# Normed tile and arena moved against the weights' address modulo 512

## The reference

```
h = rmsnorm(x) * (1 + scale) + shift        # scale, shift, gate = silu(c) @ w_ada + b_ada
proj = h @ w_in                             # retention, state-space and forgetting-attention inputs, gates
mixed = concat(retention * silu(rg), rmsnorm(ssd * silu(z)), fox * silu(fg))
x = x + gate * (mixed @ w_out)
```

```
h = rmsnorm(x) * (1 + sc1) + sh1            # both streams
conv, mlstm, attention  from  h @ w_in      # N_IN = 8976 columns
x = x + g1 * ((g_conv*conv + g_mlstm*mlstm + g_attn*attn) @ w_out)
h = rmsnorm(x) * (1 + sc2) + sh2
x = x + g2 * ((a * silu(g)) @ w_down)       # a, g = dwconv(h @ w_up), D_FF = 2816
```

## Time and profile before

| | |
|---|---|
| median of three runs | 2268.26 us |
| the profiled execution | 2270.83 us |
| its span, first to last instruction | 2269.0 us |
| mean granted TensorE clock over the span | 0.983 of full speed |
| TensorE, VectorE, ScalarE, GpSimd busy | 97%, 74%, 43%, 5% |
| DMA, GB/s over the span | 143 |

### The profile page before, as it was taken

The page is one execution under the profiler, slowest core; times in us unless marked ns, Lnnn a source line. Parts: engine busy times, 40 slices in busy tenths (PEclk is TensorE's granted clock), DMA queues, the critical chain, the costliest instruction groups (busy, mean ns, idle before and its releaser), DMA issues.

```text
span 2269.0 us, 33300 instructions
## 1 busy us (share of the span) xinstructions
PE 2195.2 (97%) x13838; PEld 1879.1 (83%) x13838; DVE 1676.1 (74%) x3037; ACT 980.0 (43%) x1568; POOL 107.8 (5%) x86
## 2 busy tenths in 40 slices
PE   5999999999999999999999999999999999999999
PEld 4898888888878887778887688867789888999999
DVE  5887879777659686647874799966459766766984
ACT  3458533485533354453222333311344546544542
POOL 0000000000000121210000000000000313000000
PEclk9999999999999999999999999999999999999999
DMA  8954378443332111116562355635442212664553
GB/s 303 330 187 130 111 254 288 130 141 106 109 93 75 56 57 38 38 43 198 172 200 93 112 191 201 201 122 180 144 113 83 85 57 66 196 204 142 180 172 121
DMA packets 280807, 324.49 MB, mean 143 GB/s; under 512 B 28496, under 2 KB 261456, under 8 KB 280528
## 3 DMA queue, kind: packets, MB, share of 16 engines
q1 hardware_dynamic: 280656, 322.36, 44.1%
HBM read 321.29 MB, written 1.05 MB: 142 GB/s over the span
## 4 chain that ended last, share of the span: by engine, by line
PE 84%; DVE 11%; ACT 2%; DMA 2%; issue 1%; POOL 0%; SPq 0%; DVEq 0%; ACTq 0%
PE ps L754 83%; DVE parts L1951 2%; DVE ring L1908 2%; DMA ring<-w_ada_t 1%; ACT w_high L1412 1%; PE ps L1203 1%; DVE arena L2506 1%; DVE arena L2052 1%; DMA ring<-w_in 1%; DVE ada_dot L1908 0%; DVE arena L2097 0%; DVE parts L2320 0%; DVE arena L2103 0%; POOL parts L1854 0%; ACT arena L1524 0%
## 5 line engine op out<-in xcount | busy, mean ns | idle before, releaser
L754 PE MATMUL ps<-parts,w_high 128*128 128x256 f32 (+1 forms) x6512 | 1142.7, 325 | 8.4 <-ACT w_high L1412 6.2
L754 PEld LDWEIGHTS ps<-parts,w_high 128*128 128x128 f32 x6512 | 970.0, 190 | 123.1 <-issue 18.6
L754 PE MATMUL ps<-parts,parts 128*128 128x256 f32 (+1 forms) x3384 | 605.1, 320 | 9.2 <-DVE parts L1951 4.3
L1412 ACT ACTIVATE w_high<-ring 128x1024 fp32r<-128x1024 f32 (+2 forms) x442 | 439.5, 1012 | 298.3 <-PE ps L754 153.0
L754 PEld LDWEIGHTS ps<-parts,parts 128*128 128x128 f32 x3384 | 503.9, 191 | 61.8 <-DVE parts L1951 7.3
L2320 DVE TENSOR_TENSOR parts<-ring,w_high 128x1024 fp32r<-128x1024 f32 (+2 forms) x282 | 320.2, 1142 | 129.9 <-ACT w_high L1412 129.6
L1908 DVE CUSTOM_DVE_ANT_0 ring<-ring,c_rows,cols 128x1024 f32<-128x1024 f32 x144 | 183.1, 1278 | 20.7 <-DMA ring<-ada_w_t 8.8
L754 PE MATMUL ps<-arena 128*64 128x256 f32 (+7 forms) x928 | 184.8, 397 | 10.8 <-ACT arena L1494 7.8
L1854 POOL TENSOR_TENSOR parts<-ring,w_high 128x512 fp32r<-128x512 f32 x80 | 107.4, 1368 | 1821.9 <-ACT w_high L1412 1821.8
L754 PEld LDWEIGHTS ps<-arena 128*128 128x128 f32 (+2 forms) x928 | 122.9, 171 | 59.2 <-issue 19.0
L2349 DVE SCALAR_TENSOR_TENSOR arena<-arena,cols 128x512 f32<-128x512 f32 (+1 forms) x240 | 159.5, 664 | 6.2
(11 more groups left out here) (266 smaller groups left out, 1856.4 us busy)
## 6 DMA issues: line engine op xcount, KB each, us to landing
ring<-w_in SPq DMA_DIRECT2D x118, 1024.0 KB, 5.3
ring<-ada_w_t SPq DMA_DIRECT2D x48, 1024.0 KB, 5.0
ring<-ffn_w_up SPq DMA_DIRECT2D x44, 1024.0 KB, 5.1
ring<-w_ada_t SPq DMA_DIRECT2D x24, 1024.0 KB, 7.0
ring<-w_out SPq DMA_DIRECT2D x16, 1024.0 KB, 5.2
ring<-ffn_w_down SPq DMA_DIRECT2D x16, 1024.0 KB, 5.2
ring<-w_out SPq DMA_DIRECT2D x16, 512.0 KB, 4.7
ring<-w_mlstm_out SPq DMA_DIRECT2D x8, 1024.0 KB, 5.2
```

The lines of the kernel that those rows point to most:

```text
L754: return tensor.matmul(o, a, b, start=first, stop=last)
L1412: scalar.activation(half_high(m), half_raw(m), ACT.Copy).then_inc(*a.step(("w_high", m)))
```

## The change

Four allocations change their size; no instruction is added, removed or reordered.

```diff
-        LINE, ASIDE = 128, 48
+        LINE, ASIDE = 128, 64
+        sb("before_normed", [P, LINE - 16])
         laid = [0]
         one_high, one_low = under([P, KT, SEQ], KT * SEQ + ASIDE), under([P, KT, SEQ], ASIDE)
         laid.append(1)
         h_low = under([P, KT, TT])
         hT = sb("hT", [P, KT, TT])
-        sb("beside", [P, LINE])
+        sb("beside", [P, LINE + 16])
         laid.append(1)
         ring_low, h_keep = under([P, RING, KT * 256]), under([P, KT, TT], RING_OPEN * KT * 256)
         ring = sb("ring", [P, RING, KT * 256])
...
-        sb("before_arena", [P, -sum(n + -n % 8 for n in widths) % LINE])
+        sb("before_arena", [P, -sum(n + -n % 8 for n in widths) % LINE + 16])
```

## The result

Over 20 runs of each, the changed kernel takes 2273.43 us (2269.5 to 2275.94) and the kernel before 2268.46 us (2263.56 to 2272.47): a ratio of 1.0017, interval 1.0011 to 1.0024. The forecast was 2241, a ratio of 0.988.

What follows compares the result with a forecast made beforehand. TensorE, busy 97%, was taken to bound the kernel by its matmul pace. Savings of 30.6 us less 1.1 ("wo1"), 1.3 (VectorE) and 1.1 (waits) gave 27.1, so 2268.3 became 2241 us; range 2206 to 2274, the forecast's own 2228 to 2255.

Steps and rivals of the forecast that it cites:

- The failed step: Moved 512-column matmuls: the same 4.4 ns saved each as at 256 columns, within 6952 x 4.4 ns = 30.6 us.
- The mis-sized term: Moved 256-column matmuls at 64 or 448: 115.6 ns, the middle of 113.3 and 117.9, 4.4 ns saved each.
- rival A: All moved matmuls: 64 and 448 lock into 113.3 ns, 39.8 us saved, 2228 us; inside the forecast's 0.53.
- 117.9 everywhere: Rival A's opposite, all moved matmuls: 6952 x 2.1 = 14.6 us less 1.1, 2255 us; inside the forecast's 0.53.
- `mixed_low` at 256: Low pass of "wo1", 256 matmuls from 192 to 256: paced as at 0, 4.4 ns lost each, +1.1 us.
- the rule of odd and even 64-byte steps: Odd 64-byte steps from the weights (64, 448) taken like 192, even ones (256) like 0.
- Phase "one": First-block phase kept at distance 192: no change, 113 to 118 ns.
- VectorE's limit: Up stage of layer 0: VectorE nearly full, so 2.7 of 4.0 us saved counts and 1.3 us is lost.
- C: Rival for the whole kernel: no effect, 0 + 1.1 us, 2269 us; chance 0.17.
- D: Rival, all second-block strips slower: 6.7 ns a matmul, up to 47.7 us, 2316, most between 2275 and 2316; chance 0.17.
- B: Rival, all moved matmuls: free of collisions at 109.3 ns, 62 us saved, 2206 us; chance 0.13.
- The rule: Skill's two independent SBUF read ports: no address matters, sum 0; the trace disagreed by 6.7 ns.

Runs made afterwards that it cites:

- e1: A program of its own, only streams of 64 split matmuls, one distance and width each, some with lead-in matmuls or VectorE work; 1110.87 us.
- e7: A program of its own, streams of 72 split matmuls behind eight lead-ins, or with passes of 8 at different distances in turn; 829.9 us.
- e9: e4's kernel plus 16 matmuls at distance 0, eight ahead of the last layer's up stage and eight ahead of its down stage; 2257.39 us, ratio 0.9944.
- e8: The kernel of e4 run again unchanged, as the neighbour of e9 and e10; 2257.67 us, ratio 0.9953.
- e4: Kernel before, with the last layer's moving tiles for 2268 matmuls of 256 columns laid 64 bytes lower, distance 448; 2258.95 us beside 2267.53, ratio 0.996.
- e10: e4's kernel with the low parts of up and down in the last layer left at distance 0, turn (192, 192, 0); 2257.57 us, ratio 0.9946.
- e2: Kernel before, with the arena's tiles alone moved by 64 bytes and hT left in place; 2272.58 us, ratio 1.0007.
- e3: Kernel before, with the normed tile hT alone moved to distance 448 and the arena left at 0; 2271.49 us, ratio 1.0002.

## Why the prediction was wrong

The measured 2273.4 us lies within the stated range, 2206 to 2274, but at the end that was there for no effect. That it lies within is luck: no part of the forecast has losses that cancel gains.

**The failed step** is "with 512 columns the same, as the excess is the same". Two widths with 13.3 ns over their streaming time at distance 0 were taken as one cost with one remedy, and the 4.4 ns won at 256 columns were booked for 3436 matmuls of 512, 15 of its 31 us before deductions. At 512 columns the rows of before held distance 0 alone, so nothing there spoke on how it moves. Measured: +2.2 ns at 64 and +6.7 at 448 (e1), and in the kernel's up stage 3.9 more on the mean of both. That is 2540 x 2.2 + 896 x 6.7 = 11.6 us lost for 15.1 won, the whole sign of the result.

**The mis-sized term** is 256 columns: 115.6 ns taken, the middle of two paces; 117.9 measured. 64 and 448 both have two paces, 113.3 and 117.8, but in the turns of 64 and 448 the slower one stood, in the last layer's up stage and in e7's (64, 64, 448) after all four lead-ins. 3516 x 2.1 = 7.4 us won instead of 15.5. The opposite of rival A, "117.9 everywhere", was right here, but for `project_values`, whose pass on `h_low` between passes at 0 ran at 113.4.

**What was right.** `mixed_low` at 256 is as at 0: 120.0 ns after 116.3, 256 x 3.7 = +0.9 us. The reason given was not: the rule of odd and even 64-byte steps fails at 128, an even number, where e1 has 118.6 and 232.1, and 64 and 192 differ with 512 columns, 228.9 and 233.3. It is the period of 256 bytes that makes 256 as 0. Phase "one" stood. VectorE's subtractions, of the changed kernel (ns min, median, max):

```profile
L1998 DVE TENSOR_TENSOR parts<-hT,parts x16: 404/406/407, 65.9 to 347.3; 128x256 fp32r<-128x256 f32 x16
L2313 DVE TENSOR_TENSOR parts<-hT,parts x32: 419/686/694, 602.2 to 2086.0; 128x512 fp32r<-128x512 f32 x24, 128x256 fp32r<-128x256 f32 x8
```

These are the values of the earlier trace rows to within 3 ns. The sum by what was measured: 11.6 - 7.4 + 0.9 = +5.1 us, and the medians differ by 5.0; the good fit is partly luck, as `h_keep`'s neighbours, pauses and the granted clock are not in it and the first block's +1.1 us is only explained in part.

**A sum that was off.** The idle time before the five forms of the earlier trace rows adds to 18.7 us, not 16, and their busy time to 1806 us, not 1600. Nothing else hangs on it.

**VectorE's limit** in the up stage of layer 0 never came into play: there was nothing to give back, as the stage grew by 3.9 us.

**The rivals.** The time lies between C's 2269 and the 2275 from which most of D runs. C was wrong in the mechanism: addresses do matter, and gains and losses nearly cancel. D's price of 6.7 ns for a low pass 64 bytes off on the other side is the value measured, but for 512 columns alone, and not by its argument, since 64 itself costs 2.2. B's floor of 109.3 is reached at no distance (e1).

**The rule.** By distance alone a stream of 512 columns goes from 226.7 to 234.4 ns and one of 256 from 113.3 to 120.0 (e1). "Doesn't steal SBUF read bandwidth" (the Trainium skill, TensorE: Matmul & The Clock Gate, section "Step-by-step: what each phase is for") therefore doesn't hold for these float32r streams in its plain form: the pace changes with the place of the loaded operand relative to the moving one, whichever of them is moved. Where in the chip the two meet, no run shows.

**Still open.** Why the period is 256 bytes and why 512 columns like distance 0 and 256 columns don't: no run looks inside the weight load. What selects the pace at 192 from one execution to the next, and what in a pause does. Whether a lead-in at distance 0 is worth time: by the pace in e9's trace the up stage wins about 1003 x 4.5 ns = 4.5 us over e8's, an estimate, less 1.9 us for the 16 added matmuls; its median doesn't show it.

## What to carry to other kernels

Where TensorE is bound by back-to-back matmuls, the address of the moving operand relative to the loaded one, modulo 256 bytes, is worth up to 3% at 512 and 6% at 256 columns, and it must be chosen for each width: here 0 for 512 and 192 for 256, the latter only in the stages that have that width (e4: 0.4% of the kernel). With 256 columns count on 117.8 rather than on 113.3, unless passes at 0 lie between. Measure every distance and width in a program of streams first (1.1 ms of chip time in e1); a pace read at one width says nothing of another. An instruction that is added to set a state also shifts the time of all that follow: compare it with one of the same length that should not set the state. Where a row exists at one value of a parameter only, its response to that parameter is unknown in sign as well, and the range must have both.

## What the runs showed of the hardware

- A stream of float32r matmuls with 128-column weight loads has a pace that depends on the distance modulo 256 bytes: 226.7 to 234.4 ns (512 columns), 113.3 to 120.0 (256). With 384 columns it goes from 173.3 to 176.7, but 192 and 448 differ.
- At 256 columns and distances 64 and 192 (modulo 256) there are two stable paces, 113.3 and 117.8 (e1, e7); at 192 either stands for more than 850 matmuls (windows of e4 and e9). Behind passes of eight at distance 0 the faster one follows in a stream alone, at 192 and 448 after each of the four lead-ins tried (e7), and e10's up stage has that turn's 115.5. A pause of about 0.5 us can switch it either way (e8).
- Moving the loaded operand by 64 bytes and not the moving one changes the pace as well: 120.0 to 113.4 in `project_values` (changed kernel).
- With 512 columns, passes at 0 in turn with passes at 64 or 448 cost 0.8 to 1.5 ns a matmul over the mean of their own paces (e2, e3, e7: 228.6 for (0, 0, 64), mean 227.4); (64, 64, 448) costs 0.2 (e7: 230.6, mean 230.4).
- With a step of 1024 instead of 512 bytes between weight tiles the paces are the same two (e7: 192 with 256 columns, 113.3 after two of four lead-ins, one of them another than with 512). VectorE's reads and writes beside a stream of 512 columns changed nothing (e1: 226.7, 228.9, 233.3 again).
